# Expert weights issued from two queues, and one feed-forward load moved ahead of the down weights

## The reference

```python
# block 1, feed-forward layer, D_FF = 2816
u = causal_dwconv(rms_norm(h) @ w_up, conv_w, conv_b)
gate, up = jnp.split(u, 2, axis=-1)
h = h + (jax.nn.silu(gate) * up) @ w_down
...
# block 2, experts: a group and two of its 8 experts for each token
y_e = (silu(x_e @ w1[e]) * (x_e @ w3[e])) @ w2[e]     # e = 0..63
out = h + sum_e weight_e * y_e                        # scattered back to the tokens
```

## Time and profile before

| | |
|---|---|
| median of the runs | 1630.36 us |
| the profiled execution: its time | 1631.2 us |
| its span, first to last instruction | 1629.4 us |
| PE busy | 1312.3 us, 81% |
| DVE, ACT, POOL busy | 373.0, 213.0, 13.9 us |
| mean granted TensorE clock | 0.911 of full speed |
| moved by DMA | 501.81 MB, of which SP's queue 500.00 MB |
| expert loads: issues, issue to landing (median) | 192, 38.1 us |

### The profile page before, as it was taken

One profiled execution on the slowest core, in us unless ns is written; L12 is line 12 of the kernel. 1 busy time (PEld: TensorE's weight loads), 2 busy tenths in 40 slices (PEclk: granted clock), 3 DMA queues, 4 the chain that ended last, 5 costly groups with the idle time before them and its releaser, 6 DMA issues.

```text
span 1629.4 us, 16426 instructions
## 1 busy us (share of the span) xinstructions
PE 1312.3 (81%) x6929; PEld 777.0 (48%) x6929; DVE 373.0 (23%) x968; ACT 213.0 (13%) x514; POOL 13.9 (1%) x26
## 2 busy tenths in 40 slices
PE   7999999999999999999676675765756757657576
PEld 4665688854478888654232232232322323323222
DVE  3344223384154200142101111110110110110101
ACT  3325223211022100111000000000000000000000
POOL 2000000000000000000000000000000000000000
PEclk9999999999999999999888788897888888878878
DMA  9431554413532444969999999999999999999997
GB/s 293 168 139 52 209 189 154 154 51 112 198 124 83 155 155 160 408 232 430 427 427 428 428 428 427 426 428 428 427 428 428 427 428 426 428 428 428 427 426 302
DMA packets 91394, 501.81 MB, mean 308 GB/s; under 512 B 6669, under 2 KB 34689, under 8 KB 65216
## 3 DMA queue, kind: packets, MB, share of 16 engines
q1 hardware_dynamic: 90560, 500.00, 75.6%
q0 software_dynamic: 768, 0.85, 0.4%
HBM read 499.78 MB, written 1.05 MB: 307 GB/s over the span
## 4 chain that ended last, share of the span: by engine, by line
PE 60%; DMA 35%; DVE 3%; ACT 1%; issue 1%; SPq 0%; ACTq 0%; DVEq 0%
DMA arena<-in_w 34%; PE ps L668 14%; PE ps L1217 9%; PE ps L988 9%; PE ps L663 5%; PE ps L1200 4%; PE ps L1237 4%; PE ps L1019 3%; PE ps L1246 2%; PE ps L843 2%; PE ps L1144 2%; DVE moe_turned L1991 1%; PE ps L1228 1%; PE ps L1059 1%; PE ps L1207 1%
## 5 line engine op out<-in xcount | busy, mean ns | idle before, releaser
L1217 PE MATMUL ps<-arena,hT 128*32 128x512 f32 x2048 | 291.5, 733 | 256.1 <-DMA arena<-in_w 253.0
L1217 PEld LDWEIGHTS ps<-arena,hT 128*32 128x32 f32 x2048 | 80.3, 131 | 466.3 <-issue 466.3
L668 PE MATMUL ps<-hT,arena 128*128 128x256 f32 x768 | 170.9, 382 | 0.1
L988 PE MATMUL ps<-hT,arena 128*128 128x256 f32 x704 | 154.4, 383 | 4.0 <-DVE arena L1666 3.0
L668 PEld LDWEIGHTS ps<-hT,arena 128*128 128x128 f32 x768 | 146.8, 192 | 22.2 <-issue 1.6
L988 PEld LDWEIGHTS ps<-hT,arena 128*128 128x128 f32 x704 | 135.0, 192 | 23.4 <-issue 3.4
L1237 PE MATMUL ps<-arena,moe_turned 128*32 128x512 f32 x1024 | 119.9, 610 | 25.1 <-DVE moe_turned L1991 25.1
L1989 DVE TENSOR_TENSOR moe_hid<-moe_hid,ps 64x512 f32<-64x512 f32 x32 | 22.1, 690 | 487.7 <-ACT moe_hid L2318 487.7
L2318 ACT ACTIVATE moe_hid<-ps 64x512 f32<-64x512 f32 x32 | 18.8, 588 | 681.6 <-PE ps L1217 681.6
L663 PE MATMUL ps<-arena,hT 128*128 128x512 f32 x192 | 84.1, 594 | 0.0
L1237 PEld LDWEIGHTS ps<-arena,moe_turned 128*32 128x32 f32 x1024 | 30.7, 111 | 89.7 <-issue 59.9
(11 more groups left out here) (371 smaller groups left out, 976.4 us busy)
## 6 DMA issues: line engine op xcount, KB each, us to landing
arena<-in_w SPq DMA_DIRECT2D x192, 2048.0 KB, 38.1
arena<-in_w_in SPq DMA_DIRECT2D x18, 2048.0 KB, 8.6
arena<-in_w_up SPq DMA_DIRECT2D x22, 1024.0 KB, 7.7
arena<-in_w_down SPq DMA_DIRECT2D x5, 2048.0 KB, 13.8
arena<-in_w_out SPq DMA_DIRECT2D x2, 2048.0 KB, 14.4
arena<-in_w_conv_out SPq DMA_DIRECT2D x2, 2048.0 KB, 7.8
arena<-in_w_attn_out SPq DMA_DIRECT2D x2, 2048.0 KB, 8.0
arena<-in_w_o SPq DMA_DIRECT2D x2, 2048.0 KB, 8.4
```

Source lines behind the costliest of these rows:

```text
L668: last = mm(o, w[:, c, q * P:(q + 1) * P], xT[:, c, :], start=(c == 0), stop=(c == KC - 1))
L988: last = mm(ps[:, 2 * s + a, g * S:(g + 1) * S], up[:, c, g, a * P:(a + 1) * P], hT[:, c, :], start=(c == 0), stop=(c == KC - 1))
L1217: last = mm(ps[k * CAP:(k + 1) * CAP, UP, :], x[:, c, (k % 2) * CAP:(k % 2 + 1) * CAP], w[:, at:at + DE], start=(c == 0), stop=(c == KC - 1))
```

## The change

Three edits. First, the loop that issues the expert units is now `load_units(eng, w2)` and runs twice: SP issues the units with k = 0 to 3, GpSimd those with k = 4 and 5 (w2), after its last small load. Every unit keeps its slot, its source, its shape and its wait. Second, the semaphore that counts a unit's landing belongs to the unit's kind and the parity of its pair (12 semaphores), not to its slot (11), and PE waits on it. Third, `up2` is issued before the wait for the turned input and the down weights, and `up3` between the three fixed down loads and `downA`.

```diff
-        moe_loaded = [sem(f"moe_loaded{i}") for i in range(NSLOT)]
+        moe_loaded = [sem(f"moe_loaded{i}") for i in range(2 * UNITS_PAIR)]
...
+        def loaded_by(unit):
+
+            pair, k = divmod(unit, UNITS_PAIR)
+            return moe_loaded[UNITS_PAIR * (pair % 2) + k], 16 * (pair // 2 + 1)
+
+        def load_units(eng, w2):
+
+            for unit in range(PAIRS * UNITS_PAIR):
+                if (unit % UNITS_PAIR >= 4) == w2:
+                    moe_wait(eng, unit)
+                    pair, k = divmod(unit, UNITS_PAIR)
+                    if pair in HALVED:
+                        load = load_half(eng, unit % NSLOT, pair, k)
+                    else:
+                        load = load_whole(eng, unit % NSLOT, k, slice(2 * pair + k % 2, 2 * pair + k % 2 + 1))
+                    load.then_inc(loaded_by(unit)[0], 16)
...
-            static_units(1, U_FFN + 2)
+            static_units(1, U_FFN + 3)
             sp.wait_ge(hT_dve, 8)
             sp.wait_ge(hT_act, 8)
             for place, lo, n in ((6, 0, 4), (7, 4, 4)):
                 sp.dma_start(arena[:, place, :].rearrange("p (a n) -> p a n", a=n), w_down[:, lo:lo + n, :]
                              ).then_inc(down_loaded, 16)
             sp.dma_start(down_at(4), w_down[:, 8:10, :]).then_inc(down_loaded, 16)
+            static_units(U_FFN + 3, U_FFN + 4)
             static_units(UNIT["downA"], UNIT["downC"])
-            static_units(U_FFN + 2, UNIT["downA"])
+            static_units(U_FFN + 4, UNIT["downA"])
             static_units(UNIT["downC"], len(UNITS))
...
+            load_units(sp, False)
...
             pool.dma_start(router_w[:, :, NG:], t["w_router_2"].rearrange("(c p) n -> p c n", p=P)).then_inc(late_in, 16)
+
+            load_units(pool, True)
...
             def wait_unit(unit):
-                pe.wait_ge(moe_loaded[unit % NSLOT], 16 * (unit // NSLOT + 1))
+                loaded, n = loaded_by(unit)
+                pe.wait_ge(loaded, n)
```

More of the change, by code:

```diff
@@ L495, in dense_loads, with load_half, load_whole, moe_wait @@
             return 16 * n
+        def load_half(eng, slot, pair, k):
+            lo = (0, 0, 2048, 2048, 0, 2048)[k]
+            src = t[("w1", "w3", "w1", "w3", "w2", "w2")[k]][2 * pair:2 * pair + 2, :, lo:lo + 2048]
+            return eng.dma_start(MOE_SLOTS[slot].rearrange("p (e n) -> p e n", e=2), src.rearrange("e p n -> p e n"))
+        def load_whole(eng, slot, k, expert):
+            src = t[("w1", "w1", "w3", "w3", "w2", "w2")[k]][expert, :, :]
+            return eng.dma_start(MOE_SLOTS[slot], src.rearrange("o p n -> p (o n)"))
+        def moe_wait(eng, unit):
+            if unit < 3:
+                eng.wait_ge(attn2_done, 1)
+            elif unit == 3:
+                eng.wait_ge(merged, 1)
+            elif unit in (6, 7):
+                eng.wait_ge(merged, 4)
+            elif unit < NSLOT:
+                eng.wait_ge(dense_used, 1 + (UNIT[{4: "ga1", 5: "wao1", 8: "wo0", 9: "wo1", 10: "wo1"}[unit]]))
+            else:
+                pair, k = divmod(unit - NSLOT, UNITS_PAIR)
+                if pair in HALVED:
+                    eng.wait_ge((up_half, up_half, up_filled, up_filled, down_half, y_filled)[k], pair + 1)
+                else:
+                    eng.wait_ge((up_filled, up_filled, up_filled, up_filled, y_filled, y_filled)[k], pair + 1)
+        def loaded_by(unit):
[6 more added lines that the diff above has]
+                    pair, k = divmod(unit, UNITS_PAIR)
+                    if pair in HALVED:
+                        load = load_half(eng, unit % NSLOT, pair, k)
+                    else:
+                        load = load_whole(eng, unit % NSLOT, k, slice(2 * pair + k % 2, 2 * pair + k % 2 + 1))
+                    load.then_inc(loaded_by(unit)[0], 16)
         @block.sync
@@ L572, in _ @@
                     for k in range(UNITS_PAIR):
-                        load_whole(k, k, bass.ds(g * 2 + k % 2, 1)).then_inc(over_loaded, 16)
+                        load_whole(sp, k, k, bass.ds(g * 2 + k % 2, 1)).then_inc(over_loaded, 16)
             for half in range(2):
```

## The result

The changed kernel takes 1644.33 us (median of four runs, 1641.93 to 1646.89) against 1630.3 us (now the median of four runs too): ratio 1.0079, 95% interval 1.0067 to 1.0092, a loss of 12.9 us (10.9 to 15.0). The forecast was 1642.3. The profiled execution took 1641.93 us with a span of 1640.2 us, so the trace shows 10.8 us of the loss in its span, and is the shortest of the four; where the other 2 us of the median lie, no kept trace shows.

The account below looks back on a forecast made before the run. PE's product chain was taken to bound the first part, the weight stream the rest from about 733 us. Costs of 9.8 us at the end and 2.1 in feed-forward gave +11.9, median 1642.3; forecast's own range 1635 to 1647, overall 1628 to 1657.

Parts of the forecast that it names:

- The second queue releases nothing earlier: Issue of expert units: moving 64 issues off SP is worth 0, bounds 1 us gain to 1 us loss.
- How two queues share, and which unit lands last: Expert stream: two queues share equally while both have work, so 189 lands last, at 1619.0 us, where 191 landed.
- down to a fifth: Last pair: even if GpSimd got only a fifth of the engines, 191 would not land behind the four up units.
- The end, +9.8: After the last landing: 12.4 us of work in place of 2.6, so +9.8 us, bounds 8.1 to 12.
- The feed-forward edit, +2.1: Feed-forward loads: up2's stall goes, new stalls come before up3 and up4; +2.1 us, bounds -3.0 to +3.5.
- PE's chain carries it whole to the start of the stream: From feed-forward layer to unit 11's issue: the +2.1 us arrives undiminished at the stream's start.
- The total, 12.9 against 11.9: Whole kernel: 9.8 at the end plus 2.1 in the feed-forward layer, 11.9 us slower, median 1642.3.
- GpSimd's units do not go slower: Rival, expert stream: GpSimd's units go through more slowly, +13 us (1655) to +56 us (1698); chance 0.15.
- Nor do two queues go faster: Rival, expert stream: two queues keep the engines fuller, -18.5 us, giving 1624 with the +11.9; chance 0.08.
- the window of 437: Expert stream: a short window at 437 against 428 GB/s, taken as the rate two queues might reach.
- The order did not stay: Rival, end of stream: landing order stays, only the feed-forward term left, 1632.5, chance 0.08; 1627.4 at its lower bound, chance 0.03.
- The feed-forward edit did not win its 3.0 us: Rival, feed-forward layer: the edit gains 3.0 us while the end still costs 9.8, 1637.2; chance within the forecast's 0.66.

Follow-up runs that it names:

- e3: Changed kernel with the old feed-forward load order and all units of the last two pairs issued by SP, against the kernel before: ratio 1.0001, +0.2 us.
- e7: Kernel with all 192 expert units issued by GpSimd in their old order, feed-forward loads as before, against the kernel before: ratio 0.9999, -0.2 us.
- e1: Changed kernel with the feed-forward loads in their old order, so only the two queues, against the kernel before: ratio 1.0069, +11.3 us.
- e4: Kernel before, SP alone, with units 190 and 191 issued ahead of 188 and 189, against the kernel before: ratio 1.0059, +9.6 us.
- e2: Kernel before with only the feed-forward edit, one queue, against the kernel before: ratio 1.0003, +0.5 us.
- e6: Kernel before with downA and downB put one each into later periods, after up3 and up4, against the kernel before: ratio 0.9978, -3.6 us.
- e5: Kernel before with up2 alone moved ahead, up3 left behind all five down loads, against the kernel before: ratio 1.0064, +10.4 us.

## Why the prediction was right, point by point

- **The second queue releases nothing earlier: right.** e3 and e7 are within 0.2 us of before, with intervals of about 2 us to either side.
- **How two queues share, and which unit lands last: right.** 191 landed 3.7 us ahead of 189. GpSimd's units took 14.4 us to land where 10 to 14 were expected. The exact share was not measured; the sum does not need it, since the order was argued to hold down to a fifth.
- **The end, +9.8: right, a little low.** The trace shows 10.2: the second half of up took 5.71 us in place of 5.34. The same 32 products of the first half had run in 3.62 us at a granted clock of 1.00; after the 5.81 us of waiting the clock was 0.50 from 1620 to 1623 us. So about 2 us of the 12.8 are clock. e1 measures 11.3 (8.8 to 13.5), e4 9.6. Shown from three sides: with the second queue, without it, and with it but in the old order.
- **The feed-forward edit, +2.1: right up to up4, wrong behind it.** The stall before up2 went and came back before up3 (e2: 4.29 us, forecast 2.2 to 3.4) and up4 (0.22 and 0.72, forecast about 2). Three things differ from the sum.
  - The load: in the changed kernel the third down load landed 14.4 us after up2 (222.1 against 199.4 + 8.3 = 207.7) and not 12.8 to 14.
  - The clock behind the stall, which the sum left out: it was 0.66 from 230 to 235 us in e2, so up3 took 15.5 to 15.7 us and not 13.8, which hid most of up4's wait. At up4 e2 was 3.7 us behind, counted from the layer's first product (64.2 us against 60.6), more than the 1.6 to 2.8 of the forecast; the changed kernel was 2.2 behind.
  - The step that failed is the last one, that "PE's chain carries it whole to the start of the stream". Unit 11 is issued 542.3 us after the layer's first product in e2, 542.5 in the changed kernel, 541.8 before: of the 3.7 and 2.2 us some 0.4 and 0.7 are left. The last section shows where the rest came back. As a time, e2 says +0.5 (-1.3 to +2.3), and the changed kernel less e1 is 1.6, a difference whose interval holds 0; neither tells 0.5 from 2.1.
- **The total, 12.9 against 11.9: in part luck.** The end cost more than its term (10.2 in the trace, 11.3 in e1, for 9.8) and the feed-forward edit probably less (0.5 for 2.1). The two misses have opposite signs. The intervals of e1 and e2 still hold the forecast terms, so the timings alone do not settle it; the traces speak for it.
- **The rivals.** GpSimd's units do not go slower: e7 puts a bound of 1.6 us on 192 of them. The Trainium skill ("DMA: Bandwidth & Descriptors", "Latency and other measured facts") calls two of the 16 engines usually slower and guesses at GpSimd's descriptors as the cause; in units of 2 MB with 16 KB rows no run here shows a cost of it. Nor do two queues go faster: 428 GB/s in both, so the window of 437 was no rate to be had. The order did not stay. The feed-forward edit did not win its 3.0 us; e6 did.

## What to carry to other kernels

When a stream of loads is the bound, the time is when it starts, its bytes, and the work behind the last landing; a change of queue leaves the bytes alone but changes which load lands last, so put last the one with the least work behind it. An in-order queue that waits for a slot holds back every load behind the wait, and what it held back then stands ahead of the next one that is wanted. A stall that is taken out must be looked for one load later, and a big load that nobody wants yet did best here (e6) in the gaps of the periods to come.

## What the runs showed of the hardware

In three traces part of a loss in the feed-forward layer was won back later, where the granted clock was higher than before. These are windows of the kernel before, of e2 and of e5, first from 215 to 250 us, then from 470 to 540 us, where none of them waits for a load (the clock is the third value from the right):

```profile
215.00:250.00 35.00, 34.87 (x162) 30.74 (x163) 10.25 (x23) 8.66 (x15) 0.00 (x0) 1.00 0.45 145
...
470.00:540.00 70.00, 65.39 (x311) 56.41 (x309) 28.35 (x70) 15.77 (x48) 0.00 (x0) 0.95 0.27 97
```

```profile
215.00:250.00 35.00, 30.48 (x133) 25.92 (x133) 10.09 (x23) 8.72 (x15) 0.00 (x0) 0.95 0.88 319
...
470.00:540.00 70.00, 65.39 (x328) 57.09 (x326) 31.68 (x75) 15.77 (x48) 0.00 (x0) 1.00 0.32 117
```

```profile
215.00:250.00 35.00, 20.89 (x87) 17.71 (x87) 6.78 (x15) 6.39 (x11) 0.00 (x0) 0.80 0.77 289
...
470.00:540.00 70.00, 65.40 (x324) 57.13 (x323) 40.50 (x81) 15.36 (x46) 0.00 (x0) 1.00 0.30 107
```

In e2 and e5 the granted clock fell below full in the first window, behind the stall before up3, and was then the full 2.4 GHz from 470 to 540 us, where the kernel before was granted 0.95, a part of the time at 1.2 GHz. At 0.95, 70 us hold some 3.5 us of clock. The timeline of PE measures it between two instructions that all kernels have, first before, then e2:

```profile
477.36 1.91 PE L1126 MATMUL ps<-consts,arena 128*128 128x128 f32 x16
540.38 34.77 PE L668 MATMUL ps<-hT,arena 128*128 128x256 f32 x160
...
480.85 1.91 PE L1127 MATMUL ps<-consts,arena 128*128 128x128 f32 x16
540.50 34.77 PE L669 MATMUL ps<-hT,arena 128*128 128x256 f32 x160
```

From one to the other it is 63.0 us before and 59.7 us in e2: 3.4 us of the 3.7 come back here. In e5 it is 59.6. The changed kernel lies between, with a clock of 0.98 and 61.1 us. In e1, e3, e4, e6 and e7 the two windows show 1.00 and 0.95, as before.

A longer stall or an earlier dip of the clock is not by itself what spares the later one. In e3 and e7 PE stood 5.04 and 5.09 us before up2, longer than e2 before up3, and the clock was 0.66 from 210 to 215 us; from 470 to 540 us they were granted 0.95 all the same, and e3 took 63.0 us between the two instructions. What decides it no run here shows, and each kernel has one trace only. What can be said is that in these traces 3.7 us lost in one stage were worth some 0.4 us at the start of the stream, and that a single execution is no measure of such a change: the runs of before spread over 8.7 us on one chip and 6.7 us on the other.

The stream of loads does not end at its full rate. In the changed kernel the mean share of the DMA engines is 0.62 from 1612 to 1616 us and 0.24 from 1616 to 1620 us, while unit 189, the last, lands at 1619.5; before it is 0.67 from 1612 to 1614.7 and 0.47 from 1614.7 to 1618. By the rates of those two windows of the changed kernel (260 and 102 GB/s) some 1.4 MB were left at 1612 us, which at 428 GB/s would be through at about 1615.4: an estimate that puts the last landing 4 us behind a stream at its full rate.
